# TensorE's pair loop rolled into a hardware loop of six pairs

## The reference

```
xn = rmsnorm(x, g_pre)
pool_y = pool_mixer(xn @ w_in[:, pool], ...)          # trailing means, windows 2/4/8/16
sb_y   = stick_breaking(q, k, v)                      # 8 heads x 128, from xn @ w_in
ml_y   = mlstm_chunkwise(q, k, v, i, f, c0, n0, m0)   # 4 heads x 256, from xn @ w_in
merged = sum over the three branches of
         sigmoid(xn @ w_in[:, gate_b]) * ((y_b * silu(xn @ w_in[:, z_b])) @ w_branch[b])
x_out  = x + rmsnorm(merged @ w_out, g_post)
```

## Time and profile before

| | |
|---|---|
| median of the runs | 2434.05 us |
| profiled execution | 2423.55 us |
| its span, first to last instruction | 2422.0 us |
| TensorE (PE) busy | 2274.7 us, 94% |
| VectorE (DVE) busy | 1471.9 us, 61% |
| ScalarE (ACT) busy | 923.9 us, 38% |
| GpSimd (POOL) busy | 244.4 us, 10% |
| mean granted clock of TensorE | 0.973 |

### The profile page before, as it was taken

How to read it: one execution, slowest core, us unless ns; L and a number is a source line. 1 busy time by engine, 2 the same in 40 slices (tenths; PEclk the granted TensorE clock), 3 DMA queues, 4 the chain that set the end, 5 groups by cost and what they waited for, 6 DMA issues and landing times.

```text
span 2422.0 us, 40440 instructions
## 1 busy us (share of the span) xinstructions
PE 2274.7 (94%) x16616; PEld 2233.8 (92%) x16616; DVE 1471.9 (61%) x1636; ACT 923.9 (38%) x1232; POOL 244.4 (10%) x301
## 2 busy tenths in 40 slices
PE   3799999999999999999999999999997898699996
PEld 3799999999999999999999999999886788699996
DVE  5867678667666666676666666655663666243333
ACT  4344334334433344444444444445541233122221
POOL 3100000000100001110000000003442111000000
PEclk7899999999999999999999999999997999899998
DMA  5244434444544444444444444466555553635322
GB/s 148 58 120 116 133 101 118 131 117 131 125 115 122 124 117 117 124 123 114 129 126 115 119 124 117 117 212 203 174 183 170 188 162 118 170 104 183 86 70 95
DMA packets 417613, 316.01 MB, mean 130 GB/s; under 512 B 11309, under 2 KB 376997, under 8 KB 415472
## 3 DMA queue, kind: packets, MB, share of 16 engines
q1 hardware_dynamic: 397456, 250.12, 37.4%
q0 software_dynamic: 20000, 63.61, 7.5%
HBM read 252.42 MB, written 61.26 MB: 130 GB/s over the span
## 4 chain that ended last, share of the span: by engine, by line
PE 86%; DVE 6%; DMA 4%; ACT 2%; issue 1%; POOL 1%; SPq 0%; DVEq 0%; ACTq 0%; POOLq 0%
PE pp L685 62%; PE pp L819 10%; PE pp L987 7%; DMA gt_lo<-gated_scratch 2%; PE M L693 2%; PE M L872 1%; PE M L902 1%; DMA raw_b<-in_w_out_dram 1%; PE M L919 1%; PE M L842 1%; PE M L785 1%; PE M L852 1%; DVE den L1867 1%; DVE xa L1427 1%; DVE XA L1750 0%
## 5 line engine op out<-in xcount | busy, mean ns | idle before, releaser
L685 PE MATMUL pp<-xa,wa_hi 128*128 128x288 f32 x7680 | 1543.6, 296 | 26.6 <-DVE wa_lo L1384 14.8
L685 PEld LDWEIGHTS pp<-xa,wa_hi 128*128 128x128 f32 x7680 | 1235.2, 188 | 29.0 <-DVE xa L1427 10.8
L685 PE MATMUL pp<-xa,wa_lo 128*128 128x288 f32 x3840 | 1131.6, 295 | 0.0
L685 PEld LDWEIGHTS pp<-xa,wa_lo 128*128 128x128 f32 x3840 | 725.9, 189 | 0.0
L1384 DVE TENSOR_TENSOR wa_lo<-raw_a,wa_hi 128x1024 fp32r<-128x1024 f32 x274 | 340.6, 1246 | 253.6 <-ACT wa_hi L1025 253.5
L1025 ACT ACTIVATE wa_hi<-raw_a 128x1024 fp32r<-128x1024 f32 x274 | 289.1, 1056 | 225.4 <-PE pp L685 218.6
L1384 DVE TENSOR_TENSOR wa_lo<-raw_r,wa_hi 128x1024 fp32r<-128x1024 f32 x136 | 173.2, 1273 | 141.6 <-ACT wa_hi L1025 141.6
L819 PE MATMUL pp<-gt_hi,wb_hi 128*128 128x288 f32 x768 | 171.9, 306 | 37.6 <-DMA gt_lo<-gated_scratch 37.6
L1025 ACT ACTIVATE wa_hi<-raw_r 128x1024 fp32r<-128x1024 f32 x136 | 143.5, 1055 | 133.5 <-PE pp L685 133.5
L819 PE MATMUL pp<-gt_hi,wb_lo 128*128 128x288 f32 x768 | 166.4, 299 | 0.0
L819 PE MATMUL pp<-gt_lo,wb_hi 128*128 128x288 f32 x768 | 166.4, 299 | 0.0
(11 more groups left out here) (278 smaller groups left out, 2137.3 us busy)
## 6 DMA issues: line engine op xcount, KB each, us to landing
raw_a<-in_w_in_dram SPq DMA_DIRECT2D x206, 512.0 KB, 5.0
raw_r<-in_w_in_dram SPq DMA_DIRECT2D x68, 512.0 KB, 4.9
z_scratch<-zs POOLq DMA_DIRECT2D x60, 576.0 KB, 3.3
raw_b<-in_w_branch_dram SPq DMA_DIRECT2D x48, 512.0 KB, 4.2
raw_b<-in_w_out_dram SPq DMA_DIRECT2D x32, 512.0 KB, 4.4
gz<-z_scratch SPq DMA_DIRECT2D x48, 288.0 KB, 4.0
gt_hi<-gated_scratch SPq DMA_DIRECT2D x6, 1152.0 KB, 10.3
gt_lo<-gated_scratch SPq DMA_DIRECT2D x6, 1152.0 KB, 13.1
```

Source lines behind the costliest of these rows:

```text
L685: i = nc.tensor.matmul(out, ws[:, slot, k, :], xa[:, o, part, k, :], start=opens and k == 0 and s == 0, stop=k == HK - 1 and s == 2, skip_ ...
```

## The change

TensorE's first 20 pairs stay written out. The other 48 become a hardware loop of eight rounds with six pairs in its body. The waits inside the body compare with values made from the loop's counter. What follows the pairs, and every other engine's program, is as before.

```diff
-LOOP_EV = 50
+LOOP_PE, LOOP_EV = 20, 50
...
-            for p in range(PAIRS):
+            for p in range(LOOP_PE):
                 hooks = {}
...
                 pair_products(At(p), hooks)
+            with pe.Fori(0, (PAIRS - LOOP_PE) // 6) as i:
+                for q in range(6):
+                    pair_products(At(LOOP_PE + q, i, 6))
             pe.wait_ge(c22_done, PAIRS)
             product(At(product_at(PAIRS).base), bank_a[1], A22, False).then_inc(wa_used, 1)
```

## The result

The changed kernel takes 2492.02 us (2491.47 to 2492.62) against 2430.81 us before, measured beside it: a ratio of 1.0263, interval 1.0248 to 1.0277. The two medians differ by 61 us. One of the four runs of before took 3484.35 us; it is in the median of 2430.81 but not in the ratio, and without it before is 2427.57 and the difference 64 us. The forecast was 2435 us with a range from 2418 to 2458.

What follows compares the result with a forecast made beforehand. The prediction took TensorE's matmul rate as the only bound. Unchanged matmuls and register waits cost 0; seven branches back at 1.6 us (fetch 3.3 less cover 1.7) add 11 us to 2423.55, giving 2435 us, range 2418 to 2458.

Steps and rivals of the forecast that it cites:

- What bounds the kernel, and that nothing is to be won: Pair phase: TensorE's matmul rate, 133.3 ns each, is the only limit; any hole moves the end by its own length.
- Register waits at no cost: Waits in the loop body: 84 register operations and the branch's per round, hidden by the sequencer's lead, cost 0.
- slower, by the waits: Rival, each product's first wait: lead lost, 0.2 us of register work bare at 336 products, 67 us, 2491 us; chance 0.05.
- Slower, by fetches: Rival, loop body: reading ahead stops after a miss, 66 packets cost 70 to 100 us, near 2510 us; chance 0.04.
- The body's beginning is gone when the branch comes: Branches back: after about 8.2 packets the body's start is no longer in the engine, so all seven branches miss.
- The cover of 1.7 us, from a lead of 2.0 to 2.1: Branches back: the sequencer's lead over the array, less about 0.4 us of branch and register work, hides 1.7 us.
- The price of the fetch, 3.3 us and a hole of 1.6: Each branch back: fetching one packet takes 3.3 us; less the cover, a 1.6 us hole, 11 us over seven.
- A branch then waits for one packet: Each branch back: TensorE waits for a single code packet, and code read in sequence afterwards costs 0.
- The prediction's own signs of being wrong: Pair phase in the profile after: holes absent, more than seven holes, or one over 3.3 us.
- For 1.6 us I take none: Granted clock after each branch's hole: no drop expected at 1.6 us; a drop would cost 1.7 us.
- the lower base: Starting time of the sum: the profiled execution, 2423.55 us, rather than the shown median of 2434.05 us.
- The rival with the long holes: Rival, branches back: fetch of 5.0 us behind weight loads plus a clock drop each, 35 us, 2459 us; chance 0.12.

Runs made afterwards that it cites:

- e4: The changed kernel with twelve pairs in the loop body and four rounds, so three branches back instead of seven: 2454.01 us, ratio 1.0095.
- e6: The kernel before, its old TensorE loop over output tiles made three rounds of four tiles, two tiles written out: 2428.77 us, single run.
- e7: The kernel before, its old TensorE loop over output tiles made two rounds of six tiles, two tiles written out: 2434.01 us, single run.
- e5: The changed kernel with the loop's head at instruction 128 of a 256-instruction block, no prefetch hint: 2443.88 us, ratio 1.0069.
- e2: The changed kernel with a prefetch hint armed each round for the branch that closes it: 2439.96 us, ratio 1.004.
- e1: The changed kernel with the loop's head placed on the first instruction of a fetched block: 2458.63 us, ratio 1.0117.
- e3: The changed kernel with 26 pairs written out instead of 20, then seven rounds of six pairs: 2450.85 us, ratio 1.0088.
- e9: The changed kernel with the loop's head at instruction 200 of a block, no prefetch hint: 2456.5 us, single run.
- e10: The changed kernel with the prefetch hint and the loop's head at instruction 0 of a block: 2444.17 us, single run.

## Why the prediction was wrong

**What bounds the kernel, and that nothing is to be won:** right. In the body TensorE passes a matmul each 133.3 ns, and every hole moved the end by its length: 62.5 us in the chain, 61 to 64 us timed.

**Register waits at no cost:** right, and more cheaply than counted (52 operations a round). The rival "slower, by the waits" is out by the window of 131.20 us and by e4. That its figure of 2491 us is within 1 us of the time measured is chance. "Slower, by fetches" is out as it was priced, since reading ahead goes on inside the body, but it named the place: after a miss it sets in again only 1.9 to 3.3 us after the branch. (The prediction counts 40 pairs of straight code as removed; they are 48 less the six of the body, 42. The sum doesn't use it.)

**The body's beginning is gone when the branch comes:** right. The branch takes 4.8 us instead of 0.21. That bodies of 3.2 and 4.8 blocks don't pay it (e6, e7) fits the body's size as the cause; no size between 4.8 and 8.08 was run.

**The cover of 1.7 us, from a lead of 2.0 to 2.1:** somewhat low. At every branch of e5 and of the changed kernel the hole is 2.2 us shorter than the branch.

**The price of the fetch, 3.3 us and a hole of 1.6:** right in the hole, for a packet that comes alone, and only for that. The fetch is 3.4 to 3.9 us and the cover 2.2, so both were too small by about 0.5 and the error cancels. e5 has this case: holes of 1.2 to 1.7 us, 12.2 us over its 7728 matmuls and 14.7 us timed, where the sum said 11. In the changed kernel the branch is 1.2 us longer, with the read-ahead set off at the last border under way at the same time.

**"A branch then waits for one packet":** this is the step that failed. I counted how many blocks the body fills and not where its head lies in one. The head is some five instructions ahead of a block's end, so that one matmul after the first wait the next block is wanted, and TensorE stands for another 3.6 to 4.15 us. The sum has no term for it, and it is the largest part: of 8.9 us a branch (the mean of the six rounds), the lone fetch is 1.5, the read-ahead beside it 1.2, the second hole 3.8, the clock 1.9, and 0.5 goes in the two restarts, each of which costs 0.25 us beyond its hole (134.65 us for 1008 matmuls in e2 and e5). e1, which has no second hole, costs 28.5 us and not 61. The prediction's own signs of being wrong showed it: fourteen holes in place of seven, seven of them over 3.3 us.

**"For 1.6 us I take none" (the clock):** right for the hole it was said of (e2, e5: no drop), wrong here, since the holes were of 2.7 and 3.8 us. The price that I read from the earlier trace rows, 1.7 us, is near the 1.9 measured; in e1 a drop cost 1.5 to 2.7.

**The base and the range.** Of the four runs of before one took 3484.35 us; the other three have a median of 2427.57, so the lower base was the right choice. The rival with the long holes took 5.0 us a branch, one fetch at its slowest and the clock. The upper end bounded the price of one fetch and left the number of fetches at one. A count of TensorE's instructions ahead of pair 20 might have shown the head's place: e3, where 2058 instructions more moved it over a border, is that count used.

The Trainium skill's rule ("Runtime: NRT & Kernel Launch", Instruction fetch mechanics: a taken branch out of the fetched pages stalls for the page) is borne out, by 4.75 to 5.13 against 0.21 us. By its 128 KiB for TensorE eight blocks would fit; the runs agree as far as they go, with 4.8 blocks kept and 8.08 not. The same section calls what is fetched a window of two pages, which the runs don't bear out for TensorE: bodies of 3.2 and 4.8 blocks were branched back to in 0.24 us at most.

## What to carry to other kernels

Before rolling a stretch of code in which one engine is the bound, set the body's instructions against the packets of the instruction queue: a body that the engine doesn't keep pays at every branch back, about the fetch less the engine's lead, and the loop wins nothing where straight code is read ahead without a wait. If it must be rolled, hint the branch and place the head in the middle of a block; if not, take few rounds with large bodies, or a body of few blocks. A hole that went with a lower clock cost 1.5 to 2.7 us more than its length here.

## What the runs showed of the hardware

- A taken branch to code that TensorE no longer holds takes 3.3 to 3.9 us with its packet alone (e5, e9) and 4.3 to 5.2 us with the read-ahead's packet under way too (the changed kernel, e1, e3, e4); to code that it holds, 0.21 us. The sequencer's lead hides 2.2 us of it.
- After such a branch TensorE passes the next block border only 4.2 to 5.9 us after the branch has ended: a second hole of 3.6 to 4.15 us with the head 5 instructions ahead of the border, of 1.5 to 2.0 us at 56, and none at 128 or 256.
- A prefetch hint works from the last block border ahead of the branch: branches of 0.35 us with the border some 150 instructions ahead, of 3.0 to 3.4 us with some 20.
- Holes of 0.9 to 2.0 us never lowered the granted clock here (e2, e5, e9, e10: 35 holes); holes of 2.5 to 3.0 us went with the lower level at 9 of 13 branches, the double ones of 2.7 and 3.8 us at all seven.
- The release that the profile names for a wait can be wrong when the wait is the sequencer's: the first hole of the changed kernel stands under "DVE wa_lo", and it was a branch.
